# One early gate unit instead of two, a reordered routing step, thirteen weight slots and position tables issued from SyncE in a two-block transformer kernel

## The reference, cut to what matters

```python
proj = h @ w_in[i] + b_in[i]
conv_out = conformer_conv(a, g, conv_w[i], conv_b[i], conv_ln_g[i], conv_ln_b[i])
attn_out = neighbourhood_attention(q, k, v, rpb[i])          # rpb: table of relative positions
mix = concat([conv_out, attn_out]) @ w_out[i] + b_out[i]
h = layer_norm(ALPHA * h + mix, ln1_g[i], ln1_b[i])
if i == 0:  f = swiglu(h, ffn_w1, ffn_w3, ffn_w2)
else:       f = moe_swiglu(h, w_router, moe_w1, moe_w3, moe_w2)   # top 2 of 8 experts per token
e = sigmoid(h @ ple_gate_w[i] + ple_gate_b[i]) * (p[i] @ ple_w[i])
h = layer_norm(ALPHA * h + f + e, ln2_g[i], ln2_b[i])
```

## Time and profile before

| | |
|---|---|
| time, median of 3 runs | 2107.55 us (2106.07 to 2116.28) |
| the profiled execution: time | 2112.75 us |
| the profiled execution: span from first to last instruction | 2111.0 us |
| mean granted clock of PE in it | 0.992 of full |
| PE busy | 2019.2 us (96%) |
| DVE busy / ACT busy | 791.4 us / 405.9 us |
| bytes moved by DMA | 506.74 MB, mean 240 GB/s |

### The profile page before, as it was taken

The page is one execution under the profiler, slowest core; times in us unless marked ns, Lnnn a source line. Parts: engine busy times, 40 slices in busy tenths (PEclk is TensorE's granted clock), DMA queues, the critical chain, the costliest instruction groups (busy, mean ns, idle before and its releaser), DMA issues.

```text
span 2111.0 us, 36869 instructions
## 1 busy us (share of the span) xinstructions
PE 2019.2 (96%) x15858; PEld 1462.9 (69%) x15858; DVE 791.4 (37%) x1796; ACT 405.9 (19%) x954; POOL 5.9 (0%) x12
## 2 busy tenths in 40 slices
PE   8999999999899999999999999999999999999887
PEld 6879999987766666666666566666744667474776
DVE  5847555596511111111011101112346354345454
ACT  1243110104210120000100000002133333124322
POOL 0000000000000000000000000000000000000000
PEclk9999999999999999999999999999999999999999
DMA  8484444444389999999999999995211111131120
GB/s 305 153 274 184 160 175 185 178 176 169 122 326 414 420 419 414 420 420 421 411 417 420 420 420 420 420 420 213 93 47 41 60 40 41 60 120 61 40 81 20
DMA packets 72373, 506.74 MB, mean 240 GB/s; under 512 B 7825, under 2 KB 9873, under 8 KB 11793
## 3 DMA queue, kind: packets, MB, share of 16 engines
q1 hardware_dynamic: 71056, 500.15, 59.1%
q0 software_dynamic: 1152, 4.19, 0.8%
HBM read 503.27 MB, written 1.05 MB: 239 GB/s over the span
## 4 chain that ended last, share of the span: by engine, by line
PE 89%; DMA 4%; DVE 4%; ACT 2%; issue 1%; DVEq 0%; SPq 0%; ACTq 0%
PE ps L469 87%; DMA work<-weights 2%; DMA ring<-weights 2%; PE ps L1256 1%; PE ps L809 1%; DVE work L2724 1%; ACT work L1877 0%; DMA xc<-x_t 0%; DVE work L2685 0%; PE ps L681 0%; DVE work L2056 0%; DVE work L2791 0%; DVE work L2681 0%; PE ps L1357 0%; DVE work L2682 0%
## 5 line engine op out<-in xcount | busy, mean ns | idle before, releaser
L469 PE MATMUL ps<-work 128*32 128x256 f32 (+8 forms) x5608 | 570.8, 383 | 21.1 <-DVE work L2736 6.3
L469 PE MATMUL ps<-work,ring 128*128 128x256 f32 (+2 forms) x2056 | 523.9, 408 | 9.7 <-DVE work L2791 5.0
L469 PEld LDWEIGHTS ps<-work 128*32 128x32 f32 (+3 forms) x5608 | 369.9, 138 | 186.0 <-issue 109.7
L469 PE MATMUL ps<-ring,work 128*32 128x256 f32 (+3 forms) x4824 | 467.3, 411 | 10.3 <-DMA work<-weights 4.0
L469 PEld LDWEIGHTS ps<-work,ring 128*128 128x128 f32 x2056 | 352.2, 192 | 148.8 <-issue 108.1
L469 PEld LDWEIGHTS ps<-ring,work 128*32 128x32 f32 (+1 forms) x4824 | 260.4, 120 | 144.3 <-issue 71.8
L469 PE MATMUL ps<-xc,ring 128*128 128x256 f32 (+1 forms) x1440 | 277.5, 352 | 5.6 <-DMA ring<-weights 3.9
L469 PEld LDWEIGHTS ps<-xc,ring 128*128 128x128 f32 x1440 | 242.0, 192 | 42.6 <-issue 7.5
L2337 DVE TENSOR_TENSOR work<-work,ps 128x256 f32<-128x256 f32 x42 | 17.7, 422 | 420.4 <-ACT work L1721 420.4
L469 PE MATMUL ps<-xc,work 128*128 128x256 f32 (+1 forms) x720 | 138.3, 350 | 0.0
L469 PEld LDWEIGHTS ps<-xc,work 128*128 128x128 f32 x720 | 120.8, 191 | 19.9 <-issue 4.6
(11 more groups left out here) (278 smaller groups left out, 1184.9 us busy)
## 6 DMA issues: line engine op xcount, KB each, us to landing
ring<-weights SPq DMA_DIRECT2D x317, 1024.0 KB, 12.6
work<-weights SPq DMA_DIRECT2D x154, 1024.0 KB, 16.4
work<-rel POOLq DMA_DIRECT2D x8, 512.0 KB, 12.8
con<-consts SPq DMA_DIRECT2D x1, 1368.0 KB, 21.3
xc<-x_t SPq DMA_DIRECT2D x1, 1024.0 KB, 8.3
xc<-ctx_t SPq DMA_DIRECT2D x1, 1024.0 KB, 26.3
out<-work SPq DMA_DIRECT2D x4, 256.0 KB, 2.1
par<-params SPq DMA_DIRECT2D x1, 872.0 KB, 9.8
```

Of the source, the lines that this page charges most:

```text
L469: ins = eng.matmul(o, lhs, rhs, start=start, stop=stop, **kw)
```

## The change

- One gate unit is computed early instead of two, and three come in the stage, in cells 3, 6 and 10.
- POOL issues no DMA any more. SP issues the tables `rel`: those of the first layer with the other inputs before unit 6, those of the second layer after unit 40, in the feed-forward part.
- `places` on PE makes the counts first and in a bank of their own, and DVE runs `by_tokens` before `places`; before `order_out` it now orders the addresses alone (64 numbers instead of 384), and the rest follows behind it.

```diff
-MOE_SLOTS = 11
+MOE_SLOTS = 13
+REL_UNIT = 40
-EARLY_GATES = 2
-GATE_CELLS = [3, 7]
+EARLY_GATES = 1
+GATE_CELLS = [3, 6, 10]
...
-            slot = (n - MOE_START) % MOE_SLOTS
+            slot = (n - MOE_START + 11) % MOE_SLOTS
...
+        spare = sb("spare", [P, 2 * UC])
+        extra += [spare[:, UC * i:UC * i + UC] for i in range(2)]
...
             def places():
+                o = fill(("counts",), 1, (s["order_out"], 1))
                 eng.wait_ge(s["chosen_out"], 1)
+                mm(o[:, 0:8], ones, rank_t[:, 0, :], True, False)
+                mm(o[:, 0:8], ones, rank_t[:, 1, :], False, True).then_inc(bank_full[1], 1)
                 o = fill(("places",), 0, (s["places_out"], 1))
                 mm(o[:, 0:8], con[:, CN.all("tri_f")], rank_t[:, 0, :], True, True)
                 mm(o[:, 8:16], con[:, CN.all("tri_f")], rank_t[:, 1, :], True, False)
-                mm(o[:, 8:16], ones, rank_t[:, 0, :], False, True)
-                mm(o[:, 16:24], ones, rank_t[:, 0, :], True, False)
-                mm(o[:, 16:24], ones, rank_t[:, 1, :], False, True).then_inc(bank_full[0], 1)
+                mm(o[:, 8:16], ones, rank_t[:, 0, :], False, True).then_inc(bank_full[0], 1)
...
+            def relative(l):
+                for r in range(ROWS):
+                    p0 = GRID_W * (r % 2)
+                    src = rel[l, :, :, ROWS - 1 - r:2 * ROWS - 1 - r, :].rearrange("c h i j -> c h (i j)")
+                    eng.dma_start(relb[p0:p0 + GRID_W, r // 2, :, :], src).then_inc(s["rel_loaded"], 16)
...
+                    relative(0)
+                elif n == REL_UNIT:
+                    eng.wait_ge(s["nbr_scored"], HEADS)
+                    relative(1)
-        @block.gpsimd
-            eng.wait_ge(s["late_loaded"], 16 * N_LATE)
-                if l:
-                    eng.wait_ge(s["nbr_scored"], HEADS * l)
...
-                link(eng.tensor_tensor(spread, one_hot.unsqueeze(1).broadcast_to([P, 6, 8, 8]),
-                                       by_expert.unsqueeze(2).broadcast_to([P, 6, 8, 8]), ALU.mult))
-                link(eng.tensor_reduce(by_rank, spread, AX.X, ALU.add))
+                link(eng.tensor_tensor(spread[:, 4], one_hot,
+                                       by_expert[:, 4].unsqueeze(1).broadcast_to([P, 8, 8]), ALU.mult))
+                link(eng.tensor_reduce(by_rank[:, 4], spread[:, 4], AX.X, ALU.add))
                 eng.tensor_copy(crowded[:, 0:EXPERTS], by_rank[:, 4]).then_inc(s["order_out"], 1)
...
                     routing()
+                    by_tokens()
                     places()
-                    by_tokens()
...
-    nc = _bacc.Bacc("TRN2", target_bir_lowering=False, num_devices=1)
+    nc = _bacc.Bacc("TRN2", target_bir_lowering=False, num_devices=1, dynamic_dma_scratch_size=512)
```

More of the change, by code:

```diff
@@ L1543, in _ @@
             eng.wait_ge(s["out_stored"], 16 * KC // 2)
-        @block.gpsimd
-        def _(eng):
-            eng.wait_ge(s["late_loaded"], 16 * N_LATE)
-            for l in range(DEPTH):
-                if l:
-                    eng.wait_ge(s["nbr_scored"], HEADS * l)
[L1553 to L1556, removed]
         @block.scalar
@@ L1682, in ple_gate @@
             def ple_gate(l, c, src, to):
-                if KC * l + c >= 2 and not (l and c in (2, 3)):
+                if KC * l + c >= 2:
                     eng.wait_ge(s["ple_out"], KC * l + c - 1)
@@ L1700, in late_gates @@
                 for f in range(2):
-                    ple_gate(1, 2 * j + f, o[:, f * T:f * T + T], silu_sb[:, 1, f, :] if j == 1 else sig_sb[:, f, :])
+                    ple_gate(1, 2 * j + f, o[:, f * T:f * T + T], sig_sb[:, f, :])
             def moe():
@@ L2220, in routing @@
                 eng.wait_ge(s["chosen_out"], 1)
+                link(eng.tensor_copy(by_expert[:, 4], con[:, CN.all("bases")]))
                 eng.wait_ge(s["gate_exp"], 2)
@@ L2230, in places @@
                 in_order = o[:, 0:16].rearrange("p (a b) -> p a b", b=8)
-                eng.tensor_tensor(slot_of, in_order, rank_t, ALU.mult).then_inc(s["dve_order"], 1)
-                order[0] += 1
-                eng.tensor_copy(counts, o[:, 16:24]).then_inc(s["places_out"], 1)
-                eng.wait_ge(s["dve_order"], order[0])
+                eng.tensor_tensor(slot_of, in_order, rank_t, ALU.mult).then_inc(s["places_out"], 1)
                 eng.wait_ge(s["places_out"], 1)
                 link(eng.tensor_scalar(slot_of, slot_of, -1.0, None, ALU.add))
+                link(eng.tensor_tensor(spread, one_hot.unsqueeze(1).broadcast_to([P, 6, 8, 8]),
+                                       by_expert.unsqueeze(2).broadcast_to([P, 6, 8, 8]), ALU.mult))
+                eng.wait_ge(s["order_out"], 1)
+                link(eng.tensor_reduce(by_rank, spread, AX.X, ALU.add))
             def by_tokens():
+                link(eng.tensor_copy(counts, tile(eng, "counts")[:, 0:8]))
                 first = con[:, CN.all("before")].rearrange("p (a b) -> p a b", b=8)
@@ L2242, in by_tokens @@
                 other, own = counts.unsqueeze(1).broadcast_to([P, 8, 8]), counts.unsqueeze(2).broadcast_to([P, 8, 8])
-                eng.tensor_copy(by_expert[:, 4], con[:, CN.all("bases")])
                 eng.tensor_tensor(more, other, own, ALU.is_gt)
@@ L2303, in scatter, with gated @@
                         add(tile(eng, "scatter", pair, part), part).then_inc(s["scattered"], 1)
-                def gated(c, by):
+                def gated(c):
                     eng.wait_ge(s["ple_copied"], 8)
@@ L2315, in gates @@
                     c = 2 * (EARLY_GATES + GATE_CELLS.index(cell))
-                    gated(c, sig_sb)
+                    gated(c)
                     eng.wait_ge(s["first_added"], 4 * cell)
@@ L2326, in moe @@
                 eng.wait_ge(s["res_ready"], 2)
-                gated(0, sig_sb)
-                gated(2, silu_sb[:, 1])
-                eng.wait_ge(s["ple_out"], KC + 4)
-                eng.tensor_tensor(res[:, 0:4, :], res[:, 0:4, :], ple[:, 0:4, :], ALU.add).then_inc(s["ple_added"], 1)
+                gated(0)
+                eng.wait_ge(s["ple_out"], KC + 2)
+                eng.tensor_tensor(res[:, 0:2, :], res[:, 0:2, :], ple[:, 0:2, :], ALU.add).then_inc(s["ple_added"], 1)
                 eng.wait_ge(s["grow_out"], 1)
```

4 lines of the change are left out of this document (1 added, 3 removed).

## The result

The changed kernel takes 2096.8 us (median of 4 runs, 2092.87 to 2098.49) against 2107.03 for the kernel before in the same comparison (4 runs, 2106.07 to 2116.28): a ratio of 0.9934, 95% interval 0.9914 to 0.9955, so 9 to 18 us faster. A second comparison gave 2097.07 against 2109.89 (5 and 15 runs), 0.9939 (0.9919 to 0.9958). The profiled execution took 2098.49 us, with a span of 2096.7.

The account below looks back on a forecast made before the run. The experts' stage was taken as bound by weight transfers, 59.9 us a cell against PE's 57.3. Stage 11.5 us (1.5 - 2.5 + 12.5) plus tables 4.2 gave 15.7, so 2107.55 became 2091.9 us; range 2088 to 2097.

Parts of the forecast that it names:

- Order sooner: Routing before the experts' stage: counts first and narrower DVE instructions let expert loads go out 1.5 us sooner (0.7 to 1.9).
- One early gate: Before the experts' stage: PE's 3.90 us wait and the half clock after it go; first step starts 13.0 us sooner.
- Transfers, 12.5 back: Start of the experts' stage: slots no longer fill, so 12.5 us of lost transfer time return; 9 to 10 slots used.
- Two slots by themselves: Experts' stage: the two added slots alone give 0 to 2 us; the early start keeps slots from filling.
- PE goes on waiting: Experts' stage: PE still waits for weights, some 5 us in place of 9.2 + 1.6.
- Tables of the second layer: End of first-layer attention: moving them removes a 2.50 us wait and 1.71 us of half clock, 4.2 us; new place costs 0.
- Of the first: First layer's tables queued ahead of unit 6: cost 0, as they may take 32 us from 35 on; upper bound 16.6.
- A: Rival, experts' stage: slots fill nevertheless, half of the 12.5 us stays lost, 2098 us; chance 0.18.
- B: Rival, experts' stage: full slots were not the cause, the 12.5 us do not return, 2104.4 us; chance 0.08.
- C: Rival, the clock: longer PE waits bring half-clock stretches costing 1.7 us each, 2094 to 2095 us; chance 0.08.
- D: Rival, slower: first layer's tables take 60 us and delay unit 6 by 28, 2120 us; with other losses, chance 0.06.
- The rule of the Trainium skill: HBM loads at about 358 GB/s: slots would hardly fill in the experts' stage, leaving -1.4 us of the sum.

Follow-up runs that it names:

- after: The profile on record of the changed kernel, unedited: profiled execution 2098.49 us, experts' stage 863.0 us.
- after_again: The changed kernel profiled once more, unedited, to see what varies between executions: experts' stage 863.6 us.
- no_early: The changed kernel with no early gate, all four gates in the stage (cells 1, 4, 7, 11), thirteen slots: stage 2.8 us longer.
- one_gate_11: The changed kernel with the experts' units through eleven slots instead of thirteen, one early gate in its own slot: stage 866.3 us against 863.3.
- the square: Four kernels, one or two early gates by eleven or thirteen slots: stage 866.3 and 863.3 us with one gate, 871.3 and 865.6 with two.

## Why the prediction was right

*The sum.* Forecast: 11.5 us in the stage and 4.2 from the tables. Measured: 874.8 - 863.3 = 11.5 in the stage (means of three profiles each), and 3.9 to 4.5 from the tables, so 15 to 16 us in the stretches that the change touches. The times say somewhat less: the two comparisons put it at 9 to 18 us, and the means of all 47 runs of the kernel before and all nine of the changed one differ by 13.7. The forecast of 2091.9 lies 5 us below the measured 2096.8, which is at the upper edge of its own range (2088 to 2097). Some 3 of these are the base of three runs, 2107.55, as larger sets of the same kernel have medians of 2109.89 to 2111.27 (11 to 17 runs). Where the other 2 went is open; the start and the clock scatter by more than that from one execution to the next.

*Order sooner, 1.5:* 1.41 at the CAST. A delay of 5.26 us moved the stage's end by 5.4; the run that took the 1.4 back moved it by 0.7, so that this small term is not confirmed to the tenth.

*One early gate:* the first step came 18.25 - 5.3 = 12.95 us sooner, forecast 13.0; the wait is gone. The half clock is gone in `after` but not for good: in `after_again` it stood from 562.9 for 3.41 us, and the first step came 11.3 sooner. The stage did not suffer from that.

*Transfers, 12.5 back:* right in size (11.8 to 13.9 lost before, nothing after) and in cause, but not in the words "the slots no longer fill". They do fill, and SP waits for them as long in total (88.7 us against 90.1); the waits are only too short for the loads under way to run out. The count of 9 to 10 slots with two under way, "a little over 11", is borne out by eleven slots losing 3.5 us and thirteen none. The unit that moves behind the order was put at 2.5 and cost 2.8 in `no_early`.

*Two slots by themselves, 0 to 2:* **the term that was mis-sized**. They are worth 3.0 us with one early gate and 5.7 with two. I reasoned from the worst moment alone, one unit's time beyond eleven; but the slots stay full all through the start, and with eleven the loads under way run low for longer than one unit (one or two under way for 7.6 us in `one_gate_11`). It left the sum untouched, since both parts are in the change.

*PE goes on waiting some 5 us:* 5.2, and 3.8 in `after_again`.

*Tables of the second layer, 4.2:* 3.9 to 4.5, and PE has no wait between 200 and 290, where they are now.

*Of the first, 0:* no wait for unit 6, but with some luck. I put the tables' transfer at 16.6 us at most, counted from 35. SP began to issue them at 8.55 in `after`, was busy with that until 31.5, and they had landed at 45.3, 36.8 us after the first issue; counted from 35, so much would have passed the 32 us that I allowed. In `after_again` SP was done at 34.8 and unit 6 went out 0.04 us behind. It landed at 51.4, and PE did not wait for it.

*The rivals.* A and B fell with the rows at 420 GB/s; that full slots were the cause is what the square shows. C (the clock) was right that half-clock stretches decide a few us, but not in that they follow from the change. D did not come. The rule of the Trainium skill (SBUF — State Buffer, Summary: rules for kernel authors) on loads at 358 GB/s would, by the estimate in the prediction, have left nothing of the stage's gain. The trace does not agree: the stretches 760 to 1000 and 1200 to 1420 ran at 418 to 420 GB/s in every profile.

## What to carry to other kernels

Where a stage is bound by its transfers, ask when the buffers are full: room and an earlier consumer are two ways to the same end, and what the one gives depends on how much of the other is there, so cost them together. A load in a queue in order is only as early as the release ahead of it; look at which instruction raises the release, not at which one is the last to read. Ask not whether a queue waits for slots, but whether the loads under way run out while it waits. Compare two profiles by stretches: two profiles of the kernel before, unedited, differ by 2.9 us up to unit 6 and by 5.5 us behind the stage.

## What the runs showed of the hardware that was not expected

- The first of the four issues of the first layer's tables held SP for 17.65 to 17.72 us in all twelve profiles that have it at the start, behind six units and six loads of inputs; the next three took 1.5 to 2.7 us, and the four at about 220 us 0.5 to 2.3 us. Only the durations are shown, not what SP waited for.
- In the stage of the changed kernel eight units landed 3.8 to 4.0 us after the one before instead of 2.48, about one in 38 (at 676.4, 767.2, 870.5 and so on to 1340.0). The transfers do not pause there: in all eight gaps the DMA engines still moved 410 to 416 GB/s. Why the landing comes late is not shown. PE's longest remaining wait for weights, 1.3 us, is no longer than what such a gap adds.
- The second block, the same code in twelve of the fourteen profiles, ran 7 to 27 us at half clock there, at places some of which change from one execution to the next; each us of it costs 0.46.
